# Extra matmuls ahead of thirty linear blocks, split bias-table builds, and moved FFN operands in a two-model transformer kernel

## The reference

```python
def first_block(...):
    x = layer_norm(x, emb_ln_g, emb_ln_b)
    for l in range(2):
        x = layer_norm(alpha * x + hybrid_mixer(x, ...), ...)            # differential + neighbourhood attention, gated conv
        x = layer_norm(alpha * x + memory_cross_attention(x, mem, ...), ...)
        x = layer_norm(alpha * x + conv_ffn(x, ...), ...)

def _layer(x, mem_2, ...):                                              # once
    h = rms_norm(x)
    proj = h @ w_in
    merged = sum over MLA, dilated and memory attention of gate * (y @ w_branch)
    x = x + rms_norm(merged @ w_o)
    x = x + rms_norm(conv_ffn(rms_norm(x), ...))
```

## Time and profile before

| | |
|---|---|
| time, median of 3 runs | 1707.86 us (1705.42 to 1713.17) |
| the profiled execution's own time | 1706.09 us |
| its span, first to last instruction | 1703.9 us |
| mean granted TensorE clock | 0.990 |
| TensorE busy, matmuls | 1642.5 us (96%), 13694 |
| VectorE, ScalarE, GpSimd busy | 1159.4, 873.1, 39.2 us |
| DMA | 305.90 MB, 180 GB/s on average |

### The profile page before, as it was taken

How to read it: one execution, slowest core, us unless ns; L and a number is a source line. 1 busy time by engine, 2 the same in 40 slices (tenths; PEclk the granted TensorE clock), 3 DMA queues, 4 the chain that set the end, 5 groups by cost and what they waited for, 6 DMA issues and landing times.

```text
span 1703.9 us, 32290 instructions
## 1 busy us (share of the span) xinstructions
PE 1642.5 (96%) x13694; PEld 1600.3 (94%) x13694; DVE 1159.4 (68%) x1720; ACT 873.1 (51%) x1317; POOL 39.2 (2%) x59
## 2 busy tenths in 40 slices
PE   9979999999999999999999999998999899999997
PEld 8978999989999999889998999998899789999997
DVE  6648778747666767877875765676565545867776
ACT  5435653646444454565365454446655445465545
POOL 1500000000000000000000000000000000000000
PEclk9989999999999999999999999999999999999999
DMA  8964466535556474446663456554535343545562
GB/s 304 256 200 143 143 211 233 200 112 198 196 176 203 158 248 151 144 144 209 234 224 107 179 176 207 178 201 137 198 125 186 100 167 131 186 149 193 179 208 88
DMA packets 82510, 305.90 MB, mean 180 GB/s; under 512 B 10656, under 2 KB 10784, under 8 KB 80192
## 3 DMA queue, kind: packets, MB, share of 16 engines
q1 hardware_dynamic: 76720, 279.44, 48.4%
q0 software_dynamic: 5648, 24.41, 4.6%
HBM read 300.59 MB, written 6.29 MB: 180 GB/s over the span
## 4 chain that ended last, share of the span: by engine, by line
PE 74%; DVE 13%; ACT 3%; issue 3%; DMA 0%; ACTq 0%; DVEq 0%
PE general L596 47%; PE general L600 12%; PE scores L638 5%; DVE weights_lo L1457 4%; PE attention_out L638 2%; PE probs_transposed L638 2%; PE scores L714 2%; ACT weights_hi L1077 2%; PE attention_out L774 1%; PE probs_transposed L733 1%; DVE x_tok L1515 1%; DVE x_tok L1512 1%; DVE softmax_stats L1620 1%; PE attention_out L816 1%; DVE xT_lo_part L1467 1%
## 5 line engine op out<-in xcount | busy, mean ns | idle before, releaser
L1457 DVE TENSOR_TENSOR weights_lo<-raw_weights,weights_hi 128x1024 fp32r<-128x1024 f32 x525 | 632.8, 1222 | 406.9 <-ACT weights_hi L1077 405.4
L1077 ACT ACTIVATE weights_hi<-raw_weights 128x1024 fp32r<-128x1024 f32 x525 | 552.4, 1057 | 397.3 <-PE general L596 224.6
L596 PE MATMUL general<-xT_hi_part,weights_hi 128*128 128x256 f32 x2432 | 685.0, 282 | 5.7 <-DVE weights_lo L1457 3.2
L596 PE MATMUL general<-xT_hi_part,weights_lo 128*128 128x256 f32 x2432 | 677.7, 279 | 0.0
L596 PE MATMUL general<-xT_lo_part,weights_hi 128*128 128x256 f32 x2432 | 677.7, 279 | 0.0
L596 PEld LDWEIGHTS general<-xT_hi_part,weights_hi 128*128 128x128 f32 x2432 | 460.7, 189 | 14.2 <-issue 9.0
L596 PEld LDWEIGHTS general<-xT_hi_part,weights_lo 128*128 128x128 f32 x2432 | 459.0, 189 | 0.0
L596 PEld LDWEIGHTS general<-xT_lo_part,weights_hi 128*128 128x128 f32 x2432 | 458.5, 189 | 0.4
L1779 DVE SCALAR_TENSOR_TENSOR exp_ring<-general,param_cols,exp_ring 128x255 f32<-128x255 f32 (+1 forms) x176 | 76.8, 478 | 47.8 <-ACT exp_ring L1243 46.3
L1243 ACT ACTIVATE exp_ring<-general,param_cols 128x256 f32<-128x256 f32 x88 | 44.9, 561 | 71.6 <-PE general L596 71.6
L1120 ACT ACTIVATE exp_ring<-exp_ring,softmax_stats 128x256 f32<-128x256 f32 (+3 forms) x56 | 29.3, 524 | 98.5 <-DVE softmax_stats L1625 98.4
(11 more groups left out here) (294 smaller groups left out, 2978.8 us busy)
## 6 DMA issues: line engine op xcount, KB each, us to landing
raw_weights<-in_stream SPq DMA_DIRECT2D x525, 512.0 KB, 4.2
attention_area<-in_ln_rows POOLq DMA_DIRECT2D x9, 1024.0 KB, 4.8
bias_scratch<-in_rpb POOLq DMA_DIRECT2D x32, 96.0 KB, 12.1
attention_area<-bias_scratch POOLq DMA_DIRECT2D x2, 1536.0 KB, 7.4
memT_hi<-memT_scratch POOLq DMA_DIRECT2D x2, 1024.0 KB, 5.3
memT_lo<-memT_scratch POOLq DMA_DIRECT2D x2, 1024.0 KB, 9.0
attention_area<-in_mem SPq DMA_DIRECT2D x1, 1024.0 KB, 5.1
z_tok<-in_x SPq DMA_DIRECT2D x1, 1024.0 KB, 8.8
```

The costliest lines, as they stand in the source:

```text
L596: ins = nc.tensor.matmul(ps[b][0:m, half * T:half * T + T], w[wk][:, half * m:half * m + m], x[xk_], start=first, stop=last, skip_group_ch ...
L1077: nc.scalar.activation(hi_half(h), raw_half(h), ACT.Copy).then_inc(*hi_done.more())
L1457: nc.vector.tensor_tensor(lo_half(h), raw_half(h), hi_half(h).bitcast(F32), ALU.subtract).then_inc(*lo_done.more())
```

## The change

1. Ahead of the first matmul of 30 linear blocks TensorE does one more, with the high weights of that block as both operands, into the bank that the block then overwrites.
2. The bias tables of layer 0 are built in `pro`, after 8 split halves in place of 12; those of layer 1 in `l0`, after the row loads of its last norm. The save of `memT` comes behind the load of layer 0's table, and the waits go with them.
3. The transposes of the second memory are done in two lots: two tiles after `("xo", 1)`, two after `("xo", 2)`; VectorE's share is parted in the same way.
4. `ffn_act` and `memory_out` begin at 320 modulo 512 in place of 448.

```diff
+BRIDGED = {
+    "pro": {("xk", 1)},
+    "l0": {("qa", 0), ("hc", 0), ("kn", 0), ("vn", 0), ("vn", 1), ("xv", 1), ("xq", 2), ("xv", 2), ("xq", 3), ("xv", 3)},
+    "l1": {("hc", 0), ("vn", 0), ("vn", 1), ("xv", 1), ("xq", 2), ("xv", 2), ("xq", 3), ("xv", 3)},
+    "post": {("c", 1), ("dq", 5), ("dk", 0), ("dk", 1), ("dk", 5), ("dv", 0), ("dv", 4), ("dv", 5), ("gate", 1),
+             ("gate", 2), ("gate", 3)},
+}
-        fa_hi, fa_lo = (sb(f"ffn_act_{k}", 4 * T, "area", c + SHIFT, F32R) for k, c in (("hi", 0), ("lo", 4 * T)))
+        fa_hi, fa_lo = (sb(f"ffn_act_{k}", 4 * T, "area", c, F32R) for k, c in (("hi", 0), ("lo", 4 * T)))
-        xo_hi, xo_lo = (sb(f"memory_out_{k}", 8 * T, "area", c + SHIFT, F32R) for k, c in (("hi", 24 * T), ("lo", 32 * T)))
+        xo_hi, xo_lo = (sb(f"memory_out_{k}", 8 * T, "area", c, F32R) for k, c in (("hi", 24 * T), ("lo", 32 * T)))
@@ linear, on TensorE
                     x = [part[:, kc, :] for part in act]
+                    if kc == 0 and key in BRIDGED[stage.name]:
+                        nc.tensor.matmul(ps[b][:, 0:T], w[0][:, 0:P], w[0], start=True, stop=True,
+                                         skip_group_check=True)
@@ TensorE, output blocks of the memory attention
-                linear(("xo", 1), XO, DC, False)
-                if l == 1:
-                    for tile in (mem2_tile0, mem2_tile1):
-                        pe.wait_ge(*tile.at(0))
-                    to_feature("mem2T", mem2)
-                for cb in (2, 3):
+                for cb in range(1, 4):
                     linear(("xo", cb), XO, DC, False)
+                    if l == 1 and cb < 3:
+                        for tile in (mem2_tile0, mem2_tile1):
+                            pe.wait_ge(*tile.at(0))
+                        for i in (2 * cb - 2, 2 * cb - 1):
+                            transposes(("mem2T", i), mem2, 2 * i)
@@ ScalarE, gate 0 of a layer
-                            act.wait_ge(*(mt_saved.at(-1) if stage.layer == 0 else mt_in.at(-1)))
+                            act.wait_ge(*(mt_saved.at(1) if stage.layer == 0 else mt_in.at(-1)))
@@ VectorE, memory_norm
-                    if cb == 2:
-                        gains("mem2T", MT)
+                    if cb >= 2:
+                        gains("mem2T", MT, pairs=(2 * cb - 4, 2 * cb - 3))
@@ GpSimd
-            pool.wait_ge(*hi_done.at(3 * SPLIT - 1))
-            for l in range(DEPTH):
-                (16 transfers of layer l)
-                if l == 0:
-                    pool.wait_ge(*when_read(("memT", DC // 2 - 1)))
-                    for k in range(2):
-                        part, copy = mem_parts(k)
-                        pool.dma_start(copy, part).then_inc(*mt_saved.more())
+            pool.wait_ge(*hi_done.at(2 * SPLIT - 1))
+            build_bias(0)
             for l in range(DEPTH):
                 stage.enter(("l0", "l1")[l])
                 pool.wait_ge(*x_ready.at(-1))
-                if l == 0:
-                    pool.wait_ge(*bias_built.at(-1))
-                    pool.wait_ge(*mt_saved.at(-1))
+                pool.wait_ge(*bias_built.at(-1))
                 pool.dma_start(bias_rows, a["bias_scratch"][l]).then_inc(*bias_in.more())
+                if l == 0:
+                    for k in range(2):
+                        part, copy = mem_parts(k)
+                        pool.dma_start(copy, part).then_inc(*mt_saved.more())
...
                 if l == 0:
+                    build_bias(1)
                     pool.wait_ge(*x_gained.at(GAINED[("l0", "ln2")] + DC // 2 - 1))
```

More of the change, by code:

```diff
@@ L136 @@
     "cols_in": (1, 1, 1, 0),
-    "bias_built": (32, 0, 0, 0),
-    "memT_saved": (2, 0, 0, 0),
+    "bias_built": (16, 16, 0, 0),
     "bias_in": (0, 1, 1, 0),
+    "memT_saved": (0, 2, 0, 0),
     "memT_in": (0, 2, 2, 0),
@@ L1467, in low, with gains @@
                 return nc.vector.tensor_tensor(dst, src, hi.bitcast(F32), ALU.subtract)
-            def gains(name, dst, between=None):
-                for i in range(DC // 2):
+            def gains(name, dst, between=None, pairs=range(DC // 2)):
+                for i in pairs:
                     reach((name, i))
@@ L2028, in mem_parts, with build_bias @@
                 return (mT_hi, mT_lo)[k][:, :].bitcast(F32), a["memT_scratch"][k]
-            stage.enter("pro")
-            pool.wait_ge(*hi_done.at(SPLIT - 1))
-            load_rows(0)
-            pool.dma_start(col[:, :], a["cols"][0]).then_inc(*cols_in.more())
-            pool.wait_ge(*hi_done.at(3 * SPLIT - 1))
-            for l in range(DEPTH):
+            def build_bias(l):
                 for h in range(RPB_H):
@@ L2043, in _ @@
                         pool.dma_start(dst.rearrange("p (j k) -> j p k", j=NJ), src).then_inc(*bias_built.more())
+            stage.enter("pro")
+            pool.wait_ge(*hi_done.at(SPLIT - 1))
+            load_rows(0)
+            pool.dma_start(col[:, :], a["cols"][0]).then_inc(*cols_in.more())
+            pool.wait_ge(*hi_done.at(2 * SPLIT - 1))
+            build_bias(0)
+            for l in range(DEPTH):
+                stage.enter(("l0", "l1")[l])
+                pool.wait_ge(*x_ready.at(-1))
+                pool.wait_ge(*bias_built.at(-1))
+                pool.dma_start(bias_rows, a["bias_scratch"][l]).then_inc(*bias_in.more())
                 if l == 0:
-                    pool.wait_ge(*when_read(("memT", DC // 2 - 1)))
                     for k in range(2):
@@ L2048, in _ @@
                         pool.dma_start(copy, part).then_inc(*mt_saved.more())
-            for l in range(DEPTH):
-                stage.enter(("l0", "l1")[l])
-                pool.wait_ge(*x_ready.at(-1))
-                if l == 0:
-                    pool.wait_ge(*bias_built.at(-1))
-                    pool.wait_ge(*mt_saved.at(-1))
-                pool.dma_start(bias_rows, a["bias_scratch"][l]).then_inc(*bias_in.more())
                 pool.wait_ge(*sc_read.at(READS[("layer", 15, 0)]))
@@ L2059, in _ @@
                 pool.wait_ge(*merged_ready.at(3))
+                if l == 0:
+                    pool.wait_ge(*mt_saved.at(1))
                 for k in range(2):
```

## The result

| | before | after |
|---|---|---|
| time, median of 7 runs | 1705.42 us | 1692.51 us |
| range of the runs | 1703.72 to 1713.17 | 1691.92 to 1697.71 |
| the profiled execution's own time | 1706.09 | 1691.98 |
| its span | 1703.9 | 1690.1 |

The ratio is 0.9924, with a 95% interval of 0.9907 to 0.9941: faster, by 13 us. The forecast was 1678, in a range of 1670 to 1697. The sign and the range held; the size did not: 13 us came of the 30 that the sum gave. The likeliest case of the forecast is the one that did not come.

The account below looks back on a forecast made before the run. TensorE was taken as the bound, busy 1642.5 of 1703.9 us. Terms -12.5 - 3.5 - 3.3 - 10.5 - 1.0 = -30.8 took 1706.1 to 1675.3 profiled; with 1.8 to the median, 1677, rounded to 1678; range 1670 to 1697.

Parts of the forecast that it names:

- likeliest case: Whole kernel: all edits pay about as summed, 1678 us, spanning 1670 to 1684; chance 0.45.
- Tables: Layer 0's first attention: the bias table lands before VectorE wants it, so the stall behind its load goes, -12.5 us.
- Lots: Second memory's transposes: parting them removes most of TensorE's 2.25 us wait and the 1.7 us half-clock loss, -3.5 us.
- 1.0 for `memory_out`: Blocks fed by `memory_out` and those following: the new address saves half of some 2 us of long steps, -1.0 us.
- they are hidden: Layer 0's FFN: layer 1's 16 table transfers cost nothing, covered by the weight stream's four halves of lead; otherwise 12 us.
- I take 17 of 20: Blocks with added matmuls: 17 of 20 turn to the short step, -6.8 us against +3.5 of added steps, net -3.3.
- rival (e): Elsewhere: added matmuls and addresses push stretches to the long step, 4.4 ns per matmul; chance 0.05 of a slower kernel.
- all pairs run at 16.33: All three FFNs: moving `ffn_act` stops the alternation and every pair takes the short 16.33 us, -10.5 us.
- rival (c): TensorE's read ports are independent, so added matmuls and addresses do nothing except cost 30 steps: 1695 us, chance 0.08.
- rival (a): FFNs: pairs keep alternating or are mixed, so everything comes but the 10.5 us: 1688 us, chance 0.22.
- (b): FFNs: they settle in a wrong mode, +3.7 to +10.7 in place of -10.5: 1692 to 1699 us, chance 0.12.
- an alignment in time between two streams of reads: TensorE's float32r steps: two read streams' timing sets short or long, and one more step shifts it; no size given.

Follow-up runs that it names:

- experiment 3: The kernel before with only the table edit and the two lots, no added matmuls, both addresses at 448: 1695.64 us, ratio to before 0.9934.
- the fourth experiment: The kernel after with layer 1's 16 table transfers sent only when the third pair's activations of layer 0's FFN are ready: 1689.48 us, ratio to before 0.9900.
- experiment 1: The kernel after without its 30 added matmuls, tables, lots and addresses as after: 1691.65 us, ratio to before 0.9915.
- experiment 12: The kernel after with layer 1's table sent late and one added matmul ahead of every linear block, 253 in place of 30: 1715.08 us.

## Why the prediction was wrong

**Tables: right.** -12.5 was forecast, -12.41 came, and layer 1's window was the measure of what is late next. The load went out at 64 us, inside the bounds.

**Lots: right.** Forecast were -3.5 for the wait and the half clock, and in the same stretch a part of the 1.0 for `memory_out`; the stretch lost 4.58, and 4.2 with `memory_out` at 448 (experiment 3). `memory_out` was not moved by itself. No wait on `memT_lo` is left among the longer ones, and the window's clock is 1.00.

**Layer 1's table: the step that failed was "they are hidden".** I read the earlier trace rows as proof, with TensorE busy for 20.00 of 20.00 us beside 14 transfers. What the row showed also, and what I passed over, was that GB/s fell from 284 to 207 while the DMA share rose: these transfers take much time for few bytes. In `pro` TensorE was busy all the same; at the beginning of an FFN, just behind a norm, it was not. The mean share of 0.57 over the FFN hid the stretch in which the stream refills. The trace of before had it, in its window over 409 to 419 us:

```profile
409.00:419.00 10.00, 9.45 (x84) 9.29 (x83) 8.76 (x11) 4.11 (x6) 0.53 (x1) 1.00 0.84 325
```

Without the table's transfers the engines are at 1.02 and 0.85 there in the fourth experiment as well (400 to 410 us). The transfers cost 1.7 us of waiting, 3 us in the medians.

**Added matmuls: the step that failed was "I take 17 of 20".** The 17 were borders where the added operation's place was taken by a down product or a whole block by token, and I applied their count to the blocks by token too, for which I had written that nothing in the trace stands. 13 of these 14 stayed long, each at +0.11. The turned ones win 0.1 at most, since the added step costs half of the 0.21 that a block can win, and a miss loses the whole 0.11. And the sum had no term for stretches further on: it counted blocks that follow directly, and left it to rival (e) that a short stretch of before could turn long, which 456 matmuls did (experiment 1, 2.0 us). Forecast was -3.3; the stretches outside the stalls and the FFNs, where most of the added matmuls stand, came out 1.6 us longer in the profiled execution, and the medians with and without them (experiment 1) can't be told apart.

**Addresses: mis-sized, since the step "all pairs run at 16.33" failed.** That the border and the address take part was right, and rival (c) falls as a mechanism: moving `ffn_act` by 128 bytes changes the step of the down product and of the blocks behind it with no other work changed (experiments 1 and 3, 4.0 us). The Trainium skill's "SBUF — State Buffer", section "Who interferes with whom", calls TensorE's two read ports independent; that sentence may hold for the ports, but the traces don't bear out the conclusion that operands' places are worth nothing. But I took a single outcome for the FFN. At 320 the gate and up blocks are all short and the down products are all long, 16.55 a pair, and so only 0.1 of the 0.32 us between the mean pair of before and the short pair came. Taken over 33 pairs that is 3 us, and the FFNs of layer 1 and the second block together gave nothing at all in the profiled execution of after, where the first blocks of each FFN ran at the long step. The forecast named pairs that alternate as its rival (a), with an FFN that gives nothing, and pairs of 16.6 to 16.97 as (b), with one that loses 3.7 or more. What came has the look of (b), no 16.33 between, and the yield of (a), nothing. The 1692.5 is 4.5 above (a)'s 1688, since the added matmuls gave nothing and the table cost its wait, neither of which (a) has. It lies in the range because that was drawn wide for (a), (b) and (c), not because a case of the forecast came: that is luck.

**What would have helped:** a pair is 96 matmuls of gate and up and 48 of the down product, and the trace of before has both kinds at both steps. So a mixed pair had its price, 96 x 113.4 + 48 x 117.8 ns = 16.54 us, 0.11 under the mean: 33 pairs give 3.6 us in place of 10.5.

**Slips in the working.** The lower end of the likeliest case, 1670, doesn't follow from its terms: with -4.5, -2 and -3.95 in the sum it is 1674.5. The "168 at 120.5" of the earlier trace rows is a mean with three gaps of 0.2 to 0.3 us in it; the step there is 117.8. Of the 15 borders behind a short down product 14 lead to blocks by feature, and all of these turned long; the fifteenth, at 1147.87 us, leads to a block by token, which stayed short. None of them changes which step failed.

**Not settled:** what in the operands' places and in time sets the step. The runs give a map (with both parts at one place, 448 alternates; 0, 128, 192, 256, 320, 384 don't; an added matmul mostly makes what follows short by feature and long by token), no mechanism. The prediction's reading, an alignment in time between two streams of reads, was tested by no run. Why the first blocks of a run and of an FFN differ between executions of one order of work was not tried.

## What to carry to other kernels

A mean DMA share over a long stretch doesn't show whether small transfers can be hidden in it: look at the 20 us in which they would be sent, and at GB/s beside the share, since transfers of a scattered kind can fill the engines with few bytes (here 724 ns for a packet of 4096 B, against 184 for the stream's). Send background transfers when the stream ahead of TensorE is full, not behind a norm where it has to refill.

When matmuls of one shape take two times with nothing waited for, price each stretch of them by itself before an edit, and count what an added operation must turn to pay for itself: here 27 of 48 steps. Then try the edit on one kind of block alone, since what turned one kind to the short step left or turned the other to the long one.

## What the runs showed of the hardware that was not expected

- Float32r matmuls of 128x128 by 256 columns go at 113.3 or 117.8 ns at the full clock. In the FFN the place of `ffn_act`, the stationary operand of the down product, decides the pattern behind the first pairs: pairs of 144 take 16.34 and 16.96 us in turn at 448 modulo 512, 16.55 at 320 and 192, 16.59 at 128 and 384, 16.64 at 0 and 256, and 16.77 with the high part at 320 and the low part at 448.
- A matmul with the same tile as both operands costs 0.11 us, behind float32 products the same (5.96 against 5.85), and ahead of every block (experiment 12) it left those by feature at the short step for 6986 of 8506 steps, and those by token at the long one for 1948 of 2198. Ten blocks by feature behind attention products or transposes were short in all four traces with it and long in all ten without it.
- Beside the bias table's transfers DMA moved 213 GB/s in all at a full share, where it reaches 415 without them, and in those 5 us the stream moved 0.79 MB in place of 1.79. The table's packets of 4096 B took 724 ns each, the stream's 184; the packets under 512 B took 3% of the engines' time.
